# Four heavy and four light expert units in a run, in place of two and two

## What is computed

```
def moe_swiglu(h, router, w_gate, w_up, w_down):
    t = h.reshape(B * S, D)
    logits = (t @ router).astype(jnp.float32)
    top_v, top_i = lax.top_k(logits, TOP_K)
    w = jax.nn.softmax(top_v, axis=-1)
    combine = jnp.sum(jax.nn.one_hot(top_i, N_EXPERTS, dtype=jnp.float32) * w[..., None], axis=1)
    out = jnp.zeros_like(t)
    for e in range(N_EXPERTS):
        out = out + combine[:, e:e + 1].astype(t.dtype) * swiglu(t, w_gate[e], w_up[e], w_down[e])
```

## Time and profile before

| | |
|---|---|
| median of 3 runs | 1365.89 us (1365.74 to 1365.95) |
| profiled execution | 1365.12 us, span of its instructions 1363.1 us |
| TensorE busy | 1346.0 us, 99% of the span |
| VectorE, ScalarE busy | 744.3 us (55%), 630.1 us (46%) |
| chain of work that ended last | TensorE 92%, VectorE 4%, ScalarE 2%, DMA 1% |
| one pair of experts, from scatter to scatter | 216.42 us |
| weights moved per pair | 96 x 896 KB = 88.08 MB |

### The profile page before, as it was taken

One profiled execution on the slowest core, in us unless ns is written; L12 is line 12 of the kernel. 1 busy time (PEld: TensorE's weight loads), 2 busy tenths in 40 slices (PEclk: granted clock), 3 DMA queues, 4 the chain that ended last, 5 costly groups with the idle time before them and its releaser, 6 DMA issues.

```text
span 1363.1 us, 16877 instructions
## 1 busy us (share of the span) xinstructions
PE 1346.0 (99%) x6782; PEld 986.7 (72%) x6782; DVE 744.3 (55%) x644; ACT 630.1 (46%) x565; POOL 28.9 (2%) x34
## 2 busy tenths in 40 slices
PE   8999999999999999999999999999999999999998
PEld 8978888888888886567666666666666666666665
DVE  6975444445654575445564555645455455553663
ACT  5855334444456465344444435434445344444442
POOL 2000000000310000000000000000000000000000
PEclk9999999999999999999999999999999999999999
DMA  9556555554542469999999999999999999999993
GB/s 323 180 181 218 191 189 192 192 190 127 182 143 94 144 227 392 420 419 419 419 392 419 419 418 391 420 372 420 420 418 407 407 396 392 420 419 419 396 419 155
DMA packets 97932, 434.83 MB, mean 319 GB/s; under 512 B 7728, under 2 KB 9888, under 8 KB 97856
## 3 DMA queue, kind: packets, MB, share of 16 engines
q1 hardware_dynamic: 97392, 433.11, 81.7%
q0 software_dynamic: 368, 0.63, 0.2%
q10 hardware_dynamic: 96, 0.03, 0.0%
HBM read 432.69 MB, written 1.05 MB: 318 GB/s over the span
## 4 chain that ended last, share of the span: by engine, by line
PE 92%; DVE 4%; ACT 2%; DMA 1%; issue 1%; SPq 0%; DVEq 0%; ACTq 0%
PE ps L1434 15%; PE ps L962 9%; PE ps L964 8%; PE ps L963 8%; PE ps L1464 8%; PE ps L1422 8%; PE ps L1424 8%; PE ps L1423 8%; PE ps L1451 4%; PE ps L1452 4%; PE ps L1453 4%; PE ps L1369 1%; PE ps L1399 1%; DMA raw<-in_lru_w_in_dram 1%; DVE wlo L1613 1%; PE ps L1360 1%
## 5 line engine op out<-in xcount | busy, mean ns | idle before, releaser
L1620 DVE TENSOR_TENSOR lows<-ring,whi 128x1792 fp32r<-128x1792 f32 x192 | 386.2, 2023 | 270.6 <-ACT whi L603 270.4
L603 ACT ACTIVATE whi<-ring 128x1792 fp32r<-128x1792 f32 x192 | 324.4, 1698 | 296.0 <-PE ps L1424 130.8
L1434 PE MATMUL ps<-ring,xl 128*64 128x448 f32 x1024 | 205.9, 545 | 1.7 <-ACT aTl L879 1.7
L1613 DVE TENSOR_TENSOR wlo<-raw,whi 128x2048 fp32r<-128x2048 f32 x73 | 166.5, 2288 | 74.0 <-PE ps L964 71.8
L1422 PE MATMUL ps<-whi,hT_hi 128*128 128x448 f32 x508 | 191.7, 377 | 0.0
L1424 PE MATMUL ps<-whi,hT_lo 128*128 128x448 f32 x508 | 185.6, 365 | 0.0
L1423 PE MATMUL ps<-lows,hT_hi 128*128 128x448 f32 x508 | 185.5, 365 | 0.0
L595 ACT ACTIVATE whi<-raw 128x2048 fp32r<-128x2048 f32 x73 | 139.3, 1915 | 87.7 <-PE ps L964 82.9
L962 PE MATMUL ps<-whi,hT_hi 128*128 128x512 f32 x384 | 152.9, 398 | 3.2 <-DVE wlo L1613 1.4
L964 PE MATMUL ps<-whi,hT_lo 128*128 128x512 f32 x384 | 149.7, 390 | 0.0
L963 PE MATMUL ps<-wlo,hT_hi 128*128 128x512 f32 x384 | 149.5, 389 | 0.0
(11 more groups left out here) (320 smaller groups left out, 1340.9 us busy)
## 6 DMA issues: line engine op xcount, KB each, us to landing
ring<-in_moe_w_gate_dram SPq DMA_DIRECT2D x128, 896.0 KB, 8.4
ring<-in_moe_w_up_dram SPq DMA_DIRECT2D x128, 896.0 KB, 8.9
ring<-in_moe_w_down_dram SPq DMA_DIRECT2D x128, 896.0 KB, 10.1
raw<-in_fox_w_in_dram SPq DMA_DIRECT2D x16, 1024.0 KB, 5.5
raw<-in_ffn_w_gate_dram SPq DMA_DIRECT2D x14, 1024.0 KB, 5.1
raw<-in_ffn_w_up_dram SPq DMA_DIRECT2D x14, 1024.0 KB, 5.1
raw<-in_ffn_w_down_dram SPq DMA_DIRECT2D x14, 1024.0 KB, 5.1
raw<-in_lru_w_in_dram SPq DMA_DIRECT2D x8, 1024.0 KB, 10.4
```

The costliest lines, as they stand in the source:

```text
L603: nc.scalar.activation(whi[:, rounded(q), 0:WIDE], ring[:, slot(i)], ACT.Copy).then_inc(hi_done, 1)
L1434: ins = mm(ps[g * HD:(g + 1) * HD, 2 + h, 0:BW], xl[:, n], ring[:, slot(i), c:c + BW], start=n == 0, stop=n == NU - 1, skip_group_check=True)
L1613: nc.vector.tensor_tensor(wlo[:, m % LR], raw[:, m % RR], whi[:, m % HR].bitcast(F32), ALU.subtract).then_inc(lo_done, 1)
L1620: nc.vector.tensor_tensor(lows[:, slot(i)], ring[:, slot(i)], whi[:, rounded(q), 0:WIDE].bitcast(F32), ALU.subtract).then_inc(lo_done, 1)
```

## The change

`RUN` becomes 4: four heavy units, then four light ones. The argument that chose the beginner of a stage goes away, and every stage begins heavy. In the opening list two steps are joined, so that the up units end with four heavy and then eight light ones. The large expert's 14 transposes now stand inside the light run of the up stage of each half, after light unit 5, with units 6 and 7 behind them. The light expert's 7 transposes of half 0 move behind the first heavy unit of G1. Both gathers keep their places behind heavy units 1 and 3 of D1, which now lie in one heavy run. The steps of ScalarE and VectorE are placed anew to match. No product, transfer or copy is added or taken away.

```diff
-RING, SPLIT, RUN = 11, 3, 2
+RING, SPLIT, RUN = 11, 3, 4
...
-def turns(steps, jobs):
+def turns(steps):
...
-        for job in jobs:
+        for job in range(2):
...
-    stage("G", 1, range(NU), LIGHT_FIRST)
-    stage("D", 0, DOWN_A, LIGHT_FIRST)
+    stage("G", 1, range(NU))
+    stage("D", 0, DOWN_A)
...
-                 ("U", 0, range(2, 4)), ("G", 1, range(4, 8)), ("U", 0, range(4, 6)), ("U", 1, range(4)),
-                 ("U", 0, range(6, 8)), ("U", 1, range(4, 8)))
+                 ("U", 0, range(2, 4)), ("G", 1, range(4, 8)), ("U", 0, range(4, 8)), ("U", 1, range(8)))
...
+                    if (job, n) == (1, 5):
+                        act_transposes(group, 0)
...
-                act_transposes(group, 0)
-                light_transposes(group, 0)
-                if group is not OPENING:
                     pe.wait_ge(m_acc, group.twice(1))
                     scatter(1)
-                for job, n in turns(range(NU), LIGHT_FIRST):
+                for job, n in turns(range(NU)):
                     if n == 0:
                         pe.wait_ge((m_tlo, l_copied)[job], group.nth(1, PAIRS))
                     half_unit(group, "G", job, 1, n)
-                    if group is not OPENING and job == 1 and n == 5:
+                    if (job, n) == (0, 0):
+                        light_transposes(group, 0)
+                    if group is not OPENING and (job, n) == (1, 1):
...
+                    if (job, n) == (1, 5):
+                        act_transposes(group, 1)
...
-                    if (job, n) == (0, DOWN_B[1]):
-                        act_transposes(group, 1)
...
                 product(group, 0)
+                lo_to(unit("G", 0, 1, 1), group)
+                act_T_lo(group, 0)
                 light_product(group, 0)
-                lo_to(unit("G", 0, 1, 0), group)
-                act_T_lo(group, 0)
+                lo_to(unit("G", 0, 1, 2), group)
```

More of the change, by code:

```diff
@@ L99, in pair_table, with place_unit, stage @@
     units, place = [], {}
[L101 to L104, removed]
+    def place_unit(kind, job, p, n):
+        place[kind, job, p, n] = len(units)
+        units.append((job, kind, p, n))
+    def stage(kind, p, steps):
+        for job, n in turns(steps):
+            place_unit(kind, job, p, n)
     if opening:
         for kind, job, few in OPENING_STEPS:
-            stage(kind, 0, few, (job,))
-    else:
-        stage("G", 0, range(NU), HEAVY_FIRST)
-        stage("U", 0, range(NU), HEAVY_FIRST)
-    stage("G", 1, range(NU), LIGHT_FIRST)
-    stage("D", 0, DOWN_A, LIGHT_FIRST)
-    stage("U", 1, range(NU), HEAVY_FIRST)
-    stage("D", 0, DOWN_B, HEAVY_FIRST)
-    stage("D", 1, range(NU), HEAVY_FIRST)
+            for n in few:
+                place_unit(kind, job, 0, n)
+    else:
+        stage("G", 0, range(NU))
+        stage("U", 0, range(NU))
+    stage("G", 1, range(NU))
+    stage("D", 0, DOWN_A)
+    stage("U", 1, range(NU))
+    stage("D", 0, DOWN_B)
+    stage("D", 1, range(NU))
     assert len(units) == PAIR_UNITS == len(place)
@@ L906, in pair @@
                     y_to_hi(1, before)
-                    hi_to(unit("G", 0, 0, 7), group)
-                    hi_to(unit("U", 0, 0, 0), group)
+                    hi_to(unit("U", 0, 0, 1), group)
                     silu(group, 0)
-                    hi_to(unit("U", 0, 0, 1), group)
+                    hi_to(unit("U", 0, 0, 2), group)
                     light_silu(group, 0)
-                hi_to(unit("G", 0, 1, 1), group)
+                hi_to(unit("G", 0, 1, 2), group)
                 act_T_hi(group, 0)
@@ L915, in pair @@
                 if group is not OPENING:
-                    hi_to(unit("G", 0, 1, 5), group)
+                    hi_to(unit("G", 0, 1, 4), group)
                     selection_T(group)
-                hi_to(unit("G", 0, 1, 7), group)
+                hi_to(unit("D", 0, 0, 1), group)
+                silu(group, 1)
+                hi_to(unit("D", 0, 0, 2), group)
                 light_silu(group, 1)
[L920 to L923, removed]
                 hi_to(unit("D", 0, 0, 6), group)
                 act_T_hi(group, 1)
+                light_T_copy(group, 1)
                 if following is not None:
-                    hi_to(unit("D", 0, 1, 2), group)
+                    hi_to(unit("D", 0, 1, 3), group)
                     gathered_hi(following)
-                    hi_to(unit("D", 0, 1, 4), group)
+                    hi_to(unit("D", 0, 1, 5), group)
                     gathered_lo(following)
@@ L1502, in opening_units @@
                             selection_transposes(group)
+                        if (kind, job, n) == ("U", 1, 5):
+                            act_transposes(group, 0)
             def first_step(group):
@@ L1506, in first_step @@
                 pe.wait_ge(m_xl, group.nth(1))
-                for job, n in turns(range(NU), HEAVY_FIRST):
+                for job, n in turns(range(NU)):
                     if n == 0 and job == 1:
@@ L1533, in pair @@
                     half_unit(group, "G", job, 1, n)
-                    if group is not OPENING and job == 1 and n == 5:
+                    if (job, n) == (0, 0):
+                        light_transposes(group, 0)
+                    if group is not OPENING and (job, n) == (1, 1):
                         pe.wait_ge(m_acc, group.twice(2))
                         selection_transposes(group)
-                for job, n in turns(DOWN_A, LIGHT_FIRST):
+                for job, n in turns(DOWN_A):
                     if n == DOWN_A[0]:
@@ L1546, in pair @@
                     half_unit(group, "U", job, 1, n)
-                for job, n in turns(DOWN_B, HEAVY_FIRST):
+                    if (job, n) == (1, 5):
+                        act_transposes(group, 1)
+                for job, n in turns(DOWN_B):
                     if job == 1 and n == DOWN_B[0]:
@@ L2125, in pair @@
                     y_to_lo(1, group.twice(0))
-                    lo_to(unit("U", 0, 0, 1), group)
+                    lo_to(unit("U", 0, 0, 2), group)
                     dve.wait_ge(m_acc, group.twice(0))
@@ L2130, in pair @@
                 product(group, 0)
+                lo_to(unit("G", 0, 1, 1), group)
+                act_T_lo(group, 0)
                 light_product(group, 0)
[L2132 to L2133 removed]
+                lo_to(unit("G", 0, 1, 2), group)
                 if group is not OPENING:
                     accumulate(1, group)
[L2136 removed]
+                    lo_to(unit("G", 0, 1, 4), group)
                     if following is not None:
                         one_hot(group)
[L2139 removed]
+                lo_to(unit("U", 0, 1, 2), group)
                 light_sum(group, 0)
[L2141 removed]
+                lo_to(unit("U", 0, 1, 7), group)
                 product(group, 1)
+                lo_to(unit("D", 0, 0, 5), group)
+                act_T_lo(group, 1)
                 light_product(group, 1)
[L2144 to L2146 removed]
+                lo_to(unit("D", 0, 1, 2), group)
                 light_sum(group, 1)
                 if following is not None:
[L2149 removed]
+                    lo_to(unit("D", 0, 1, 5), group)
                     light_rows(following)
```

2 lines of the change are left out of this document (1 added, 1 removed).

## The result

The changed kernel takes 1344.17 us, median of 4 runs (1343.61 to 1344.74), against 1365.92 us for the kernel before beside it. The ratio is 0.9841, 95% interval 0.9824 to 0.9858. It is faster by 21.7 us, where 14.4 were forecast: the time lies 7.3 us under the forecast and 4.3 us under the range. The profiled execution took 1343.61 us. One execution of a kernel further down, the changed kernel with its down units in an even order, took 1467.27 us at a mean granted clock of 0.849, and is left out of that kernel's median.

What follows compares the result with a forecast made beforehand. TensorE's own order of work was taken as the bound, transfers a close second. Three pairs at 3.49 us (10.5) plus 3.9 for the opening pair gave 14.4 us off 1365.89: 1351.5 us, range 1348.5 to 1357.

Steps and rivals of the forecast that it cites:

- the term of the light runs: In pairs 2 to 4, fewer light runs save net 9 x 0.16 = 1.44 us a pair, down units priced alike.
- fewer starts: In pairs 2 to 4, fewer run beginnings save 2.20 us for heavy and 1.44 us for light runs a pair.
- the moved transposes and scatter: Half 1's transposes, moved behind light units, cost 0.21 us a pair; the second scatter, also moved behind them, 0.20 us.
- the stall: In DOWN_A's last heavy unit, a 0.38 us step waiting for a late low part goes: 0.26 us a pair credited.
- The wait before G1: Opening pair: TensorE's 1.70 us wait shrinks to about 0.6 us, for VectorE's aT_lo; 1.1 us saved.
- Rival B: The transfer queue becomes the bound: a pair takes 214.3 us if losses double, about 1356 us in all; chance 0.12.
- A: The forecast itself: steps between runs are paid per run and halve; 1351.5 us, range 1349 to 1354.5; chance 0.78.
- The store of 4.4 us: At U1's heavy unit 6, time in hand against late transfers, 8.2 us less 3.8 for rounding; nothing charged.
- C: No gain: ten or so waits of 0.3 us a pair where stages meet eat it; 1364 to 1367 us; chance 0.04.
- D: Slower: the fourth heavy unit of each run is late; 1375 us if it takes 5.4 us; chance 0.04.
- Q: Follow-up theory, not in the prediction: the transfer queue has become the bound, its late landings make TensorE's waits.

Runs made afterwards that it cites:

- the kernel of 1372.35 us: The changed kernel with the down stages alone back in runs of two, the place of one ScalarE call left as it was: 1372.35 us, ratio 1.0048.

## Why the prediction was wrong where it was

**The step that failed** is the term of the light runs, by the sentence "I use the price of G and U units for the down units as well". It gave 0.16 us for each light run saved. For gate and up units that held. For down units a run of two cost 3.58 us and not 3.16, so each pair of runs merged gave 0.95. The size follows from the code and one row: the four units of the earlier trace rows put 3584 columns on each half, so a column costs (6.16 - 0.16) / 3584 us = 1.67 ns. The fuller half of a run of two has 2048 columns, 3.43 + 0.16 = 3.59 us; measured, 3.58. A run of four is even, 3584 columns, 6.16; measured, 6.21. The trace of before had the 3.58, which the prediction did not use. (The Trainium skill, "TensorEngine Tiling (Array Packing)", section "Key Properties", says that tiles operate independently and can run products in parallel. The runs agree, and add what unevenness costs: 3.58 us with 2048 and 1536 columns, 3.16 with 1792 on each.)

**The terms that held.** Without the limit of the queue, a pair took 209.81 us. The forecast's 212.9, less the 3.2 missed, is 209.7. So fewer starts, the moved transposes and scatter, and the stall sum up as forecast. Term by term (starts in the timelines of the kernel before and of the one with less data, pair 2 to 3), light units save 4.61 us: the 1.44 of the forecast and the 3.16 that were missed. Heavy units, the stall included, save 2.23 where 2.46 was forecast, and the moved transposes and scatter cost 0.23 where 0.41 was. That these two errors cancel is luck. The second comes from reading lengths off the chain: by their starts in the timeline of before, the 14 transposes behind heavy units take 1.80 us, not 1.71, and the second scatter 2.62, not 2.45. The timeline of TensorE in U1 and DOWN_B of pair 2, and at the end of DOWN_A, in the kernel after:

```profile
855.73 1.99 PE L1399 MATMUL ps<-ident,gt 128*128 128x128 f32 x14
857.65 3.23 PE L1434 MATMUL ps<-ring,xl 128*64 128x448 f32 x16
860.81 0.50 PE L1451 MATMUL ps<-whi,aT_hi 128*128 128x512 f32 x1
...
818.07 0.28 PE L1453 MATMUL ps<-whi,aT_lo 128*128 128x256 f32 x1
818.19 0.40 PE L1451 MATMUL ps<-whi,aT_hi 128*128 128x512 f32 x1
```

Transposes behind light units: 857.65 - 855.73 = 1.92. The two light units behind them: 860.81 - 857.65 = 3.16, so a light run does pay its start again. The step of 0.38 us in DOWN_A is 0.12. A cycle of four and four was to take 16.1 us. In the chain of the kernel after, two heavy runs with a light one between them begin at:

```profile
915.13 0.40 PE ps L1422
...
931.22 0.40 PE ps L1422
```

16.09 us. The down stages alone in runs of two cost 214.36 - 209.81 = 4.55 us a pair; 4 x 0.95 for the light runs and 4 x 0.20 for the heavy ones is 4.6.

**The opening pair.** The wait before G1 was forecast at 0.6 us, for VectorE:

```profile
565.26 0.47 PE L1422 MATMUL ps<-whi,hT_hi 128*128 128x448 f32 x1 [0.66 <-DVE aT_lo L2098]
```

It came: 0.66 us, for VectorE.

**Rival B, the queue,** had a chance of 0.12 and came true beside A, at another size. (A and B have 0.78 and 0.12; their sum is 0.90, not the 0.91 given for faster.) It was weighed for a pair of 212.9 us, with 0.9 us to spare. With the 3.2 us that were missed TensorE could do 209.8, and the queue needs 88.08 MB / 420 = 209.7 without a break. So it had to bind: a pair takes 211.12 us, 88.08 MB at 417 GB/s. It cost 1344.2 - 1338.2 = 6.0 us. The store of 4.4 us that was charged with nothing did not cover it: the wait before the light transposes is there in the first pair already, and is the longest there, 1.9 us. "I charge nothing" was right only for the gain as forecast.

**The sum again:** 14.4 forecast, + 4 x 3.16 = 12.6 for the down units, - 6.0 for the queue, is 21.0 us; measured, 21.7. Two errors of opposite sign, and the range, built for A and B one at a time, did not hold them. C and D did not come: no low part of a fourth heavy unit is among TensorE's waits in the kernel after.

**Why a pair takes 211.1 us and not 209.7.** The queue does not pause. What the DMA engines moved from scatter to scatter, 736.18 to 947.30, in the kernel after:

```profile
GB/s 411 424 419 417 423 416 417 423 417 416 422 418 417 425 416 420 421 420 418 420 417 422 418 418 420 420 418 422 419 416 421 420 417 416 420 418 425 416 413 425
DMA packets 13866, 88.45 MB, mean 419 GB/s; under 512 B 1539, under 2 KB 1539, under 8 KB 13852
```

88.45 MB at 419 GB/s are 211.1 us. The forecast's 209.7 took 420 GB/s, the rate of the best stretches, and only the weights' 88.08 MB. Half of the 0.37 MB beside them is on the queues that load instructions; what the other half is was not traced.

**What stays open.** Of the two theories for the waits, Q is shown by the transfers made smaller, by this rate, and by the 211.1 us to which a pair comes back in three kernels whose ScalarE and VectorE work in different orders. But that order does decide where the lateness comes out, and 2 to 3 us could be had from it; where in the kernel these 2 to 3 us are saved was not taken apart.

## What to carry to other kernels

Price each kind of unit from its own rows, even where two kinds move the same bytes and columns: where products go to two halves of the array, add up the columns that a whole run gives to each. When a bound has less than 1% to spare, ask what it does if the gain turns out larger than forecast, too. And where an engine's queue is written by hand, every change of order needs the places of the waits behind it looked through: six calls in the wrong places cost 15 us, and one of them made 10 us of waits.

## What the runs showed of the hardware

Products on the two column halves run side by side over more than one unit: a run of four light down units whose halves are even only as a whole took 6.21 us, against 6.16 for units even in themselves, and giving each half its products in blocks cost only 0.05 us a run.

TensorE's clock, at 2.4 GHz in the work around, fell behind some waits. Three stretches, each with a wait of TensorE in it: in the kernel of 1372.35 us, 5.2 us before the light transposes of the first pair; in the second measurement of the changed kernel, 2.3 us at the same place; in the first run with the copy and the light product moved, 0.7 us behind the scatter of pair 3. The granted clock is the number behind POOL's 0.00:

```profile
655.00:665.00 10.00, 5.55 (x19) 4.71 (x19) 6.16 (x4) 3.85 (x3) 0.00 (x0) 0.66 1.01 418
```

```profile
655.00:660.00 5.00, 4.85 (x19) 4.11 (x20) 3.18 (x3) 2.50 (x2) 0.00 (x0) 0.66 1.03 424
```

```profile
945.00:955.00 10.00, 9.27 (x34) 7.36 (x34) 7.34 (x5) 6.83 (x5) 0.00 (x0) 0.83 1.02 422
```

These are means of stretches that are partly at the full level and partly at the lower one of 1.2 GHz. In the first two, products of 512 columns behind the wait start 0.43 us apart, where they start 0.23 apart at the full level. In the kernel of 1372.35 us, the work from the light transposes to the next light unit takes 5.74 us in the first pair and 5.06 in the second (behind a wait of 1.8 us), against 3.47 in the third: 2.3 and 1.6 us on top of the waits. But the length of the wait alone does not decide it: in the first measurement of the changed kernel 1.9 us at the same place left the clock at its full level. What does decide it, no run shows. The page's 40 slices can't tell: a 9 stands for 90% or more, and the page of the kernel of 1372.35 us has a 9 in all of them. It has to be read from short stretches.
